# Decode attention as steps behind the projection's blocks, stores on ScalarE's queue, late turning of queries and keys

## The reference

```python
z = rms_norm(h, norm_w) @ w_in            # split into dq, dk, dv, dg, gq, gk, gv, gg, ga
dq = rms_norm(dq per head and half, q_norm_w); dk = rms_norm(dk ..., k_norm_w)
# prompt: causal, 4 heads, two score maps m = 0, 1 per head
s = einsum('bqhmd,bkhmd->bhmqk', q, k) * 64**-0.5 + rel_bias
a = softmax(s); p = a[:, :, 0] - lam * a[:, :, 1]; o_d = p @ v
# sample: the same against 32 cached pages of 128 positions per sequence, named by page_table, and the new rows
kp = cache_k[layer, page_table]; vp = cache_v[layer, page_table]
o_g, S = gla_chunk over chunks of 128
mix = [rms_norm(o_d) * silu(dg), rms_norm(o_g) * silu(gg)]
y = h + mix @ w_out                       # and the new keys, values and GLA states are outputs
```

## Time and profile before

| what | number |
|---|---|
| runs | 1262.85, 1264.79, 1266.5 us |
| span of the profiled execution | 1259.8 us (no separate time is given for it) |
| mean granted TensorE clock | 0.925 |
| busy share PE, DVE, ACT, POOL | 82, 46, 39, 20% |
| HBM read, written | 174.41, 19.60 MB |

### The profile page before, as it was taken

How to read it: one execution, slowest core, us unless ns; L and a number is a source line. 1 busy time by engine, 2 the same in 40 slices (tenths; PEclk the granted TensorE clock), 3 DMA queues, 4 the chain that set the end, 5 groups by cost and what they waited for, 6 DMA issues and landing times. The chain is left out here.

```text
span 1259.8 us, 27242 instructions
## 1 busy us (share of the span) xinstructions
PE 1038.3 (82%) x9055; PEld 868.5 (69%) x9055; DVE 584.6 (46%) x1430; ACT 490.0 (39%) x1383; POOL 254.2 (20%) x399
## 2 busy tenths in 40 slices
PE   4999999999999487879878887467788836777998
PEld 4999999997999466556655654155667625664886
DVE  4755522302222134443443443277878458868221
ACT  5644314613424223333333432156767345533110
POOL 0000000000000222343434341222211159800000
PEclk9999999999999799999999998558999967787999
DMA  5312332212111699999999999530000052102221
GB/s 169 93 38 95 106 122 80 82 34 76 53 49 49 215 386 338 385 387 387 387 387 387 387 387 169 148 111 9 17 10 13 1 175 74 51 26 69 97 89 60
DMA packets 106820, 195.21 MB, mean 155 GB/s; under 512 B 14406, under 2 KB 48652, under 8 KB 106732
## 3 DMA queue, kind: packets, MB, share of 16 engines
q1 hardware_dynamic: 85716, 126.03, 30.8%
q0 software_dynamic: 20480, 67.13, 14.3%
q10 hardware_dynamic: 536, 0.89, 0.2%
HBM read 174.41 MB, written 19.60 MB: 154 GB/s over the span
## 5 line engine op out<-in xcount | busy, mean ns | idle before, releaser
L843 POOL DMA_DIRECT2D vraw<-in_cache_v x256 | 137.6, 537 | 667.7 <-issue 663.8
L512 PE MATMUL pz<-wh,xTh 128*128 128x256 f32 (+1 forms) x864 | 248.7, 288 | 0.0
L512 PE MATMUL pz<-wh,xTl 128*128 128x256 f32 (+1 forms) x864 | 244.3, 283 | 0.0
L512 PE MATMUL pz<-wl,xTh 128*128 128x256 f32 (+1 forms) x864 | 244.2, 283 | 0.0
L925 PE MATMUL pk<-ident,kraw 128*128 128x128 f32 x1024 | 136.7, 291 | 57.0 <-DMA kraw<-in_cache_k 54.0
L925 PEld LDWEIGHTS pk<-ident,kraw 128*128 128x128 f32 x1024 | 121.8, 150 | 70.9 <-DMA kraw<-in_cache_k 62.0
L863 DVE COPY kt<-pk 128x512 f32<-128x512 f32 x128 | 82.9, 687 | 183.1 <-PE pk L925 182.1
L512 PEld LDWEIGHTS pz<-wh,xTh 128*128 128x128 f32 (+1 forms) x864 | 160.6, 186 | 1.6 <-issue 1.2
L512 PEld LDWEIGHTS pz<-wh,xTl 128*128 128x128 f32 (+1 forms) x864 | 160.7, 186 | 0.0
L512 PEld LDWEIGHTS pz<-wl,xTh 128*128 128x128 f32 (+1 forms) x864 | 160.5, 186 | 0.0
L643 DVE SCALAR_TENSOR_TENSOR wl<-wraw,nw,wh 128x256 fp32r<-128x256 f32 x112 | 52.3, 482 | 117.1 <-ACT wh L358 116.2
(11 more groups left out here) (241 smaller groups left out, 1857.5 us busy)
## 6 DMA issues: line engine op xcount, KB each, us to landing
kraw<-in_cache_k SPq DMA_DIRECT2D x256, 256.0 KB, 9.6
vraw<-in_cache_v POOLq DMA_DIRECT2D x256, 256.0 KB, 5.7
wraw<-in_w_in SPq DMA_DIRECT2D x14, 1024.0 KB, 5.6
out<-nat SPq DMA_DIRECT2D x32, 128.0 KB, 1.8
xb<-in_x_prompt SPq DMA_DIRECT2D x7, 512.0 KB, 3.6
xr<-in_x_prompt SPq DMA_DIRECT2D x7, 512.0 KB, 3.5
out<-xr SPq DMA_DIRECT2D x7, 512.0 KB, 2.6
val_d<-nat SPq DMA_DIRECT2D x16, 128.0 KB, 1.8
```

The source lines that it names most:

```text
L512: ins = pe.matmul(z_at(u)[0:r, 0:CB], a[:, k, P * i:P * i + r], b[:, c % 2, k, :], start=(n == 0), stop=(n == 3 * KT - 1))
L843: pool.dma_start(vraw[:, g % VR, n, :], cache_v.rearrange("a n p h d -> (a n) p (h d)")[bass.ds(page, 1)] .rearrange("o p c -> (o p) c")). ...
```

## The change

The projection and the decode attention become one block. The instructions of decode are written once per engine as a generator of 665 steps (eight in a tick, a tick being one group of four pages), with no hardware loop. After each projection block an engine goes on to the step that `steps_at` names: none until the last v blocks, then 4 steps behind each of 18 blocks, then the rest evenly over 62 blocks, 9.6 steps each.

```diff
+            paced = [u for u in uses if u[0] == "t" or u[0] == "n" and u[1:] >= (4, 4)]
+            def steps_at(u):
+                if u not in paced:
+                    return 0
+                n, slow = paced.index(u) + 1, paced.index(("n", 6, 4))
+                if n <= slow:
+                    return GRP * n
+                return GRP * slow + (PAUSE - GRP * slow) * (n - slow) // (len(paced) - slow)
...
-NZ = 4
+NZ = 3
...
+        KR, VR, TR = 6, 8, 6
...
+            for r in range(NB + 2):              # decode_pe
+                kb, b, bb = row_of(r)
+                for t in range(ticks(r)):
+                    keys_here = kb is not None and t < G
+                    if keys_here:
+                        turn_keys(kb, t, 0)
+                    yield
+                    if kb is not None:
+                        if t == 0:
+                            new_scores(kb, b)
+                        else:
+                            scores_c(kb, b, t, 0)
+                    yield
...
+                    if b is not None and t >= 1:
+                        values_c(b, t - 1)
+                    if bb is not None and t == 0:
+                        values_c(bb, G)
+                    if b is not None:
+                        turn_probs(kb, b, t)
+                    yield
```

```diff
+            def px_free(scores, turned, added):
+                if scores:
+                    pe.wait_ge(sc_out, scores)
+                if turned:
+                    pe.wait_ge(pt_out, turned)
+                if added > 0:
+                    pe.wait_ge(od_added, added)
...
+                    if s >= 3:
+                        third(s - 3)
+                    if 2 <= s < NN + 2:
+                        store(s - 2)
+                    if s < NN:
+                        go_act(steps_at(("n", c, i)))
```

In the prompt attention values, gates, queries and keys are loaded tile by tile, and PE turns queries and keys of the next tile in units h = 1 and h = 2 of the running one:

```diff
+                def prepare(x):                  # PE
+                    kind, i = x
+                    n = rq(i) if kind == "k" else (P if i < TILES - 1 else P // H)
+                    pe.wait_ge(qk_in[i % 2], 32 * (i // 2 + 1))
+                    wait_bank(pe, x)
+                    for h in range(H):
+                        ins = pe.transpose(turn_bank(x)[:, h * P:h * P + n],
+                                           qk[0:n, i % 2, 0 if kind == "q" else 1, h * P:(h + 1) * P], ident[0:n, 0:n])
+                    ins.then_inc(turned_done, 1)
...
+                def keys_lo(i):                  # DVE
+                    n = rq(i)
+                    dve.wait_ge(turned_copied, turn_no[("k", i)] + 1)
+                    for m in range(2):
+                        ins = dve.tensor_tensor(ks[own[1 - m], m, :, P * i:P * i + n],
+                                                turn_bank(("k", i)).rearrange("p (h t) -> p h t", h=H)[own[m], :, 0:n],
+                                                ks[own[m], m, :, P * i:P * i + n].bitcast(F32), ALU.subtract)
+                    ins.then_inc(klo_done, 1)
```

More of the change, by code:

```diff
@@ new lines, in hymba_kernel @@
+        selq = area.take("selq", [P, H, TS])
+        m01 = area.take("m01", [R, 2])
+        mx = area.take("mx", [P, RG])
+        lsum = area.take("lsum", [P, RG])
+        stat = area.take("stat", [P, 8])
+        by_page = area.take("by_page", [R, GRP])
+        negmax, coef, partial = stat[:, 0:1], stat[:, 1:2], stat[:, 2:3]
+        row_stat, sign_lam = stat[0:R, 3:4], stat[0:R, 4:5]
+        pk, px, po = bank[:, 6:8, :], bank[:, 4, :], bank[:, 5, :]
+        k_in = [sem(f"k_in{n}") for n in range(KR)]
@@ new lines, in decode_sp, with load_key @@
+        def decode_sp(sp):
+            def load_key(p):
+                if p >= KR:
+                    sp.wait_ge(kt_done, p - KR + 1)
+                page = sp.value_load(pages[0:1, p:p + 1], min_val=0, max_val=POOL - 1)
+                sp.dma_start(kraw[:, p % KR, :],
+                             cache_k.rearrange("a n p h d -> (a n) p (h d)")[bass.ds(page, 1)]
+                             .rearrange("o p c -> (o p) c")).then_inc(k_in[p % KR], 16)
+            sp.wait_ge(pages_in, 16)
+            for p in range(KR):
+                load_key(p)
+            for r in range(NB + 2):
+                kb, _, _ = row_of(r)
+                for t in range(ticks(r)):
+                    for n in range(GRP):
+                        yield
+                        if kb is not None and t < G:
+                            p = kb * NPAGES + t * GRP + n + KR
+                            if p < NP:
+                                load_key(p)
+                        yield
@@ new lines, in decode_pool, with load_value @@
+        def decode_pool(pool):
+            def load_value(p):
+                if p >= VR:
+                    b, g = (p - VR) // NPAGES, (p - VR) % NPAGES // GRP
+                    pool.wait_ge(pv_done, b * RG + g + 2)
+                page = pool.value_load(pages[0:1, p:p + 1], min_val=0, max_val=POOL - 1)
+                pool.dma_start(vraw[:, p % VR, :],
+                               cache_v.rearrange("a n p h d -> (a n) p (h d)")[bass.ds(page, 1)]
+                               .rearrange("o p c -> (o p) c")).then_inc(v_in[p % VR], 16)
+            pool.wait_ge(pages_in, 16)
+            pool.wait_ge(skew_out, 16 * H)
+            for r in range(NB + 2):
+                _, b, _ = row_of(r)
+                for t in range(ticks(r)):
+                    for n in range(SUBS):
+                        if b is not None and t >= 1 and n < GRP:
+                            load_value(b * NPAGES + (t - 1) * GRP + n)
+                        yield
@@ L181, in hymba_kernel @@
             LOGS = GA + 1
+            BLOCKS = [c for c in range(len(KINDS)) if c != GA]
+            wslot = lambda c: BLOCKS.index(c) % 2
             CH = [(0, 384), (384, 384), (768, NTOK - 768)]
@@ L324, in _ @@
                 link = [0]
+                stores = {k: (to, KINDS.index(k)) for k, to in
+                          (("q", q_d), ("gv", val_g), ("dg", gate_d), ("gg", gate_g))}
                 def linked(ins):
@@ L2084, in hymba_kernel @@
+        with ExitStack() as st:
+            m_ = Area(nc, FREE, SB_HIGH)
+            woh = m_.take("woh", [P, KT, D], F32R)
+            wol = m_.take("wol", [P, KT, D], F32R)
+            mh = m_.take("mh", [P, 2, KT, P], F32R)
+            ml = m_.take("ml", [P, 2, KT, P], F32R)
+            xr = m_.take("xr", [P, 2, D])
+            pY = [bank[:, n, :] for n in range(4)]
             xr_in = [sem(f"xr_in{n}") for n in range(2)]
```

2008 lines of the change are left out of this document (1031 added, 977 removed).

## The result

The changed kernel takes 1318.61 us (median of four runs, 1318.01 to 1326.2) against 1265.64 for the kernel before, measured beside it: 1.044 times as long, 95% interval 1.0408 to 1.0473. The forecast was 1237, with a range of 1155 to 1310. The profiled run took 1319.09 us, 1.7 more than its span.

A forecast was written before the change was run, and what follows sets the result against it. It took projection as TensorE-bound and decode as mostly DMA-bound, each leaving idle what the other lacks. Merged stage 775 + prompt attention 218 + GLA 130 + output 109 = 1232, + 5 = 1237 us; range 1155 to 1310.

The forecast's parts named there:

- 5 us added between span and median: Whole kernel: about 5 us between the profiled span and the median, carried over onto the 1232 us span.
- decode's DMA floor: Decode attention before the change: a DMA stage for most of its 395 us, with DMA share 1.03 from 434 to 780.
- the stores' issue: Merged stage: about 112 block stores, 50 us of issue on ScalarE, hidden by its idle time except one 0.45 us piece.
- 715 forecast: Merged stage: PE's work if it never waits, 415 projection + 248 decode groups + 35 tile switches + 17 per-row work.
- the sum: Merged stage: 715 us of PE work plus 60 us of waits, making 775 against 816 for the two stages before.
- 32 + 12 forecast: Merged stage: PE waits for key copies, 32 us in groups without a projection block between, 12 us behind 36 blocks.
- the price of the keys' wait: Prompt attention: VectorE waits for ScalarE's keys' high part; 2 x 0.63 plus 2 x 0.61, 2.5 us a tile, +1 taken.
- the relief of VectorE: Prompt attention: low parts of queries and keys taken off VectorE; counted in full, the bound is -18 us.
- The start: Prompt attention: load, two turnings, copy and five splits before the first score, +4.5 us (2 to 8).
- The dense merge: Rival, merged stage: idle engines hide all handovers, 700 us there, 200 in the prompt stage, total 1144 to 1180; chance 0.18.
- The in-order rival: Merged stage: PE waits for copies behind block evacuation and stores; 2.0 to 2.5 us a group, total 1305 to 1337; chance 0.23.
- The third rival: Prompt attention eats the gain: keys' wait and PE transposes count in full, total 1262, no change that can be told; chance 0.07.

The follow-up runs named there:

- the fifth experiment: Changed kernel with decode steps ahead of the projection block's own evacuation, store and next weights' split on ScalarE and VectorE: 1268.7 us, 1.0026 times the kernel before.
- five edits: Changed kernel with broadcast stores apart, keys' low part a unit later, whole scores, whole ticks, decode steps ahead of block results: 1222.17 us.

## Why the prediction was wrong

Of the 82 us between 1237 and 1318.61, 54 lie in the merged stage and 33 in the prompt attention. The GLA came 2 us shorter, and of the 5 us added between span and median only 1.7 were there in the profiled run.

*Right.* That decode's DMA floor goes, that key pages land in time from a ring of 6, that GLA and output stay, and that the stores' issue is hidden. PE's work at full clock: 715 forecast, 716 by the estimate above (693.9 + 22). That this fits to 1 us is in part luck. A tick without waits takes about 4.6 us, where the sum used 4.42; this is some 10 us in 64 ticks, so other terms were too high by about as much; which ones was not measured. The waits for copies came near in sum, 32 + 12 forecast and 39 measured, and that is luck too, since the reason was another (below).

*Wrong in the merged stage: 775 forecast, 829 measured.* 26 us more idle time and 28 more of busy time.
- The broadcast store of the biases was not in the sum at all. It is moved from decode, which waited for cached pages, into the projection, where three result buffers stand between a store and PE. The prediction counted the issue of the block stores on ScalarE's queue, and not what the broadcast stores on SP's queue do to them: 16.9 us idle, some 10 us gained by parting them.
- The sum has no term for the clock: PE's work after a wait was priced at full clock. By the estimate above 27 us of the 28 are the same work at the half clock, and 20 of them go with the waits in the fifth experiment. No run held the clock apart from the waits; that the one follows the other is read from rows (1.04 against 0.59 us for four transposes) and from that experiment's two differences, 32 us idle and 20 us busy.
- The copies: the amount was near, the reason not. The prediction laid 32 us to groups without a block between. With the steps ahead 16.2 us of that stay; the other half, and the long single waits up to 3.0 us, came from what stands in front of the copy on VectorE, which is ScalarE's gate chain and the weights' split. The prediction had that chain for ScalarE's copy alone.
- Value pages, counted at 0, cost 7.4 us in six waits, all between 791 and 821 us, in the last ticks of the stage. The cause was not followed.

*Wrong in the prompt attention: +12.5 forecast, +46 measured.* The step that failed is the price of the keys' wait: the two operations on each engine, 2.5 us a tile, of which +1 was taken because the relief of VectorE would nearly cancel it. The keys' low part waits not for ScalarE's two operations but for everything ahead of them: PE turns the keys at the end of its unit, behind the values. Behind the first tile's 11.7 us, VectorE waits 5 us a tile. Part of that is no loss, since the combine would have waited too (13.3 us of the 40 when the low part was moved). Moving it gave 26 us, some 3 us in each of eight tiles, so nothing cancelled. The start was 8.6 us later, not 4.5: the load after the meeting of all engines (7.7 us of wait) and POOL's four operations in a row (8.9) were priced too low together. The cause of the remaining 12 us or so of the stage is open.

*The rivals.* The dense merge is out for this kernel, though with five edits the merged stage comes to 757 us. The in-order rival had the sign, the kind of mechanism and the point: it was to decide from 88 us of stalls, and 86 were measured, with 27 more by the clock. Its price of 2.0 us a group and more was not reached (86 / 64 = 1.3); its time, 1305 to 1337, came out by way of the prompt attention, where the same mechanism stood a second time, so the time is in part luck. The third rival had the prompt attention's sign, with +28 for it, and not its size.

## What to carry to other kernels

When work of two kinds shares an in-order engine, ask of each instruction who waits for it and how much cover it has: the copy that PE waits for within a microsecond goes ahead of results that have a whole block of time. Two such reorderings, with nothing else changed, turned 4.4% slower into 1.8% faster. Price a wait by the whole list ahead of the producer, on the producer's own engine and on the one before it. Then add what PE may lose at the lower clock after it: 27 us here, beside 86 us idle.

## What was not expected of the hardware

- Removing 32 us of PE's idle time shortened the same 6,900 PE instructions by 20 us (721.05 to 700.79): twelve stretches at the half clock, 65.97 us, became three, 27.32 us.
- Four broadcast stores, each of one partition's row to 128 rows, took 16.70 us together to issue. A block store on another queue landed 18.6 us after its issue (median 2.0), and a later one took 9.03 us to issue. From 100 to 140 us the DMA share was 0.83 at only 90 GB/s.
- Key pages of 256 KB landed in 3.9 us at a DMA share of 0.67, against 9.6 at 1.03.
- Two low parts on POOL took 3.44 us and two on VectorE beside them 2.36, against 6.15 for four on POOL.
